# First modulation by slices of 128 output features, woven into the first two up tiles

## The reference

```python
def _rms(x, g):
    xf = x.astype(jnp.float32)
    y = xf * lax.rsqrt(jnp.mean(xf * xf, axis=-1, keepdims=True) + EPS)
    return y.astype(x.dtype) * g

def _modulate(xn, shift, scale):
    return xn * (1.0 + scale) + shift

def _swiglu(xm, w_in, w_out):
    a, u = jnp.split(xm @ w_in, 2, axis=-1)
    return (jax.nn.silu(a) * u) @ w_out
...
        ml = (jax.nn.silu(c) @ ada_w[l] + ada_b[l]).reshape(B, N_MOD, 1, D)
        mc = (jax.nn.silu(c_ctx) @ ada_w[l] + ada_b[l]).reshape(N_MOD, 1, 1, D)
        x = x + 0.5 * ml[:, 2] * _swiglu(_modulate(_rms(x, ffn1_norm[l]), ml[:, 0], ml[:, 1]), ffn1_w_in[l], ffn1_w_out[l])
        h = h + 0.5 * mc[2] * _swiglu(_modulate(_rms(h, ffn1_norm[l]), mc[0], mc[1]), ffn1_w_in[l], ffn1_w_out[l])
```

## Time and profile before

| | |
|---|---|
| median of 3 runs | 2353.45 us (2352.1 to 2355.32) |
| the profiled execution's own time | 2351.35 us |
| its span | 2349.6 us |
| TensorE busy | 2305.8 us, 98% |
| VectorE, ScalarE busy | 1577.8 us, 1143.3 us |
| DMA | 403.60 MB, mean 172 GB/s |

### The profile page before, as it was taken

How to read it: one execution, slowest core, us unless ns; L and a number is a source line. 1 busy time by engine, 2 the same in 40 slices (tenths; PEclk the granted TensorE clock), 3 DMA queues, 4 the chain that set the end, 5 groups by cost and what they waited for, 6 DMA issues and landing times.

```text
span 2349.6 us, 34192 instructions
## 1 busy us (share of the span) xinstructions
PE 2305.8 (98%) x13974; PEld 1942.9 (83%) x13974; DVE 1577.8 (67%) x2399; ACT 1143.3 (49%) x1692; POOL 24.4 (1%) x65
## 2 busy tenths in 40 slices
PE   7999999999999999999999999999999999999998
PEld 4887887888888787888888987888888888888887
DVE  4677433657665777667776678676676676876766
ACT  4222233446534355445545468654464455875544
POOL 0001000010000000000000000000000000000000
PEclk9999999999999999999999999999999999999999
DMA  7468322433522234654555544445545554434553
GB/s 308 179 232 323 143 90 90 153 116 145 192 91 73 75 122 159 239 190 169 196 219 194 209 147 146 157 179 190 187 179 198 217 206 180 157 140 177 183 196 125
DMA packets 59316, 403.60 MB, mean 172 GB/s; under 512 B 8269, under 2 KB 8805, under 8 KB 11672
## 3 DMA queue, kind: packets, MB, share of 16 engines
q1 hardware_dynamic: 52992, 384.33, 44.5%
q10 hardware_dynamic: 3840, 9.20, 1.1%
q0 software_dynamic: 2336, 7.96, 1.0%
HBM read 400.37 MB, written 2.67 MB: 172 GB/s over the span
## 4 chain that ended last, share of the span: by engine, by line
PE 90%; DVE 5%; ACT 2%; DMA 1%; issue 1%; SPq 0%; ACTq 0%; DVEq 0%
PE pair L558 86%; DVE ring_parts L2444 1%; PE pair L968 1%; DMA ring<-in_stream 1%; PE pair L656 1%; PE pair L1124 1%; PE pair L917 1%; ACT arena L2030 0%; DVE rows L2566 0%; ACT xT L1602 0%; DVE arena L3006 0%; PE pair L956 0%; DVE X L2572 0%; DVE xT_parts L2359 0%; ACT mix_high L1672 0%
## 5 line engine op out<-in xcount | busy, mean ns | idle before, releaser
L558 PE MATMUL pair<-xT_parts,ring_high 128*128 128x512 f32 x2112 | 747.5, 395 | 4.6 <-DVE xT_parts L2346 2.0
L558 PE MATMUL pair<-xT_parts,ring_parts 128*128 128x256 f32 (+2 forms) x2448 | 692.8, 298 | 1.4 <-DVE xT_parts L2359 1.4
L2432 DVE TENSOR_TENSOR ring_parts<-ring,ring_high 128x2048 fp32r<-128x2048 f32 x195 | 444.2, 2281 | 137.9 <-ACT ring_high L1659 137.7
L558 PEld LDWEIGHTS pair<-xT_parts,ring_parts 128*128 128x128 f32 (+1 forms) x2448 | 460.4, 188 | 41.4 <-issue 7.7
L558 PEld LDWEIGHTS pair<-xT_parts,ring_high 128*128 128x128 f32 x2112 | 384.5, 188 | 81.9 <-issue 2.8
L1659 ACT ACTIVATE ring_high<-ring 128x2048 fp32r<-128x2048 f32 x197 | 375.6, 1910 | 66.9 <-DMA ring<-in_stream 66.8
L1710 ACT ACTIVATE arena<-pair 128x512 f32<-128x512 f32 x110 | 65.6, 596 | 263.6 <-PE pair L558 263.6
L2444 DVE TENSOR_TENSOR ring_parts<-ring,mix_high 128x1024 fp32r<-128x1024 f32 x144 | 169.1, 1217 | 32.4 <-ACT mix_high L1672 32.2
L1672 ACT ACTIVATE mix_high<-ring 128x1024 fp32r<-128x1024 f32 x144 | 143.3, 1048 | 69.2 <-DMA ring<-in_stream 65.9
L558 PE MATMUL pair<-ring_parts,xT_parts 128*128 128x512 f32 (+1 forms) x448 | 174.0, 388 | 1.8 <-DVE ring_parts L2444 1.5
L558 PE MATMUL pair<-ring_parts,g_high 128*128 128x512 f32 x440 | 172.2, 391 | 0.2 <-issue 0.2
(11 more groups left out here) (441 smaller groups left out, 3837.3 us busy)
## 6 DMA issues: line engine op xcount, KB each, us to landing
ring<-in_stream SPq DMA_DIRECT2D x330, 1024.0 KB, 4.8
xn<-in_mods SPq DMA_DIRECT2D x14, 1024.0 KB, 4.9
arena<-in_mods SPq DMA_DIRECT2D x14, 1024.0 KB, 4.9
arena<-in_compress SPq DMA_DIRECT2D x8, 1024.0 KB, 6.8
gateB<-gate_rows POOLq DMA_DIRECT2D x4, 512.0 KB, 8.2
xn<-maximum_rows POOLq DMA_DIRECT2D x8, 256.0 KB, 3.6
arena<-in_bT ACTq DMA_DIRECT2D x1, 1536.0 KB, 9.3
bias_scratch<-bias_row POOLq DMA_DIRECT2D x1, 1536.0 KB, 8.9
```

Of the source, the lines that this page charges most:

```text
L558: m = pe.matmul(o, l, r, start=start, stop=stop)
L2432: ins = dve.tensor_tensor(out=ring_r[:, slot].rearrange("p a b -> p (a b)")[:, cols], in0=w[:, cols], in1=high[:, slot, cols], op=ALU.subt ...
```

## The change

The modulation weights are laid out anew: slice k (1 MB) holds, for all 1024 inputs, shift and scale of the 128 features of block k, so a feature block is done as soon as its slice is in. The eight slices no longer pass the ring; they have places of their own in the arena, in xn and in the ring's high parts. SP's queue loads x, ctx, slice 0, chunks 0 and 1, slices 1 to 7, chunks 2 and 3. For each slice TensorE does eight products of 256 columns over four groups of 32 partitions (the k blocks summed in fours), VectorE copies the result, and two products with `pick` (three additions of identity pieces) sum the four groups and bring them onto partitions; bias and gain are applied by two small VectorE operations. The rows are scaled by 1/rms ahead of the turning (`rooted_rows`), so the turning is a plain transpose. Up tiles 0 and 1 run slice by slice, both on the same feature block, with the next slices' products, transposes and picks between. Squares are over whole rows of 1024. Ahead of all this TensorE does 24 products of 64 x 64 constants (`awake`). The wait `FIRST_CONSTS` covers four loads (cT, ident, gains, biasM); the square-root table is loaded right behind the Silu; the bias rows and the clearing of their places go behind the first tile. Semaphores that became superfluous are merged (masks; the last rows' step).

```diff
+        rooted_rows = gateB
+        slices = [room(2048 * k, KD, S) for k in range(4)] + [
+            room(18 * N, KD, S), xn[:, :, :].rearrange("p a (b c) -> p (a b) c", c=S),
+            room(17408 + 2 * CW * N, KD, S), room(17408 + 3 * CW * N, KD, S)]
...
-            for j in range(SLOTS):
+            def first_load(j):
                 sp.dma_start(ring[:, j], t["stream"][j]).then_inc(loaded[j], 16)
-            turns, whole = NCH // SLOTS, (QUAD + MOD_STEPS + 2) // SLOTS + 1
+            def slice_load(k):
+                sp.dma_start(slices[k], t["slices"][k]).then_inc(slice_in[k][0], 16)
+            sp.dma_start(X[:, 0:2, :], t["x"]).then_inc(inputs, 16)
+            sp.dma_start(X[:, 2:4, :], t["ctx"]).then_inc(ctx_in, 16)
+            slice_load(0)
+            first_load(0)
+            first_load(1)
+            for k in range(1, 6):
+                slice_load(k)
+            for j in range(2):
+                sp.wait_ge(loaded[j], 16)
+                slice_load(6 + j)
+            for j in range(2, 4):
+                sp.wait_ge(loaded[j], 16)
+                first_load(j)
+            sp.wait_ge(mod_full, 6)
+            sp.dma_start(mod_w[0], t["mods"][0]).then_inc(aside_loaded[0], 16)
+            turns, whole = NCH // SLOTS, (MOD_STEPS + 2) // SLOTS + 1
             for n in range(SLOTS, SLOTS * whole):
                 sp.wait_ge(read[n % SLOTS], n // SLOTS)
                 sp.dma_start(ring[:, n % SLOTS], t["stream"][n]).then_inc(loaded[n % SLOTS], 16)
-                f = n - QUAD - 3
+                f = n - 3
                 for m in mod_chunks(f) if f >= 0 else ():
                     if m >= 2:
                         sp.wait_ge(aside_read[m % 2], m // 2)
+                    else:
+                        sp.wait_ge(mod_full, 5)
...
+            def slice_products(k):
+                pe.wait_ge(*slice_in[k])
+                if k >= 2:
+                    pe.wait_ge(mod_row, k - 1)
+                at = k % 2 * S
+                for kd in range(KD):
+                    g = kd % 4
+                    mm(bank[4][32 * g:32 * g + 32, at:at + S], scT[:, kd, :], slices[k][:, kd, :], kd < 4, kd >= 4,
+                       mod_full if kd == KD - 1 else None)
+            def slice_turn(k):
+                if k >= 2:
+                    pe.wait_ge(x_whole, k - 1)
+                for t_ in range(4):
+                    if k == 0:
+                        pe.wait_ge(rstd_done, t_ + 1)
+                    m = pe.transpose(bank[6 + k % 2][:, t_ * P:(t_ + 1) * P], rooted_rows[:, t_, k * P:(k + 1) * P],
+                                     ident[:, :])
+                m.then_inc(x_turned, 1)
+            def slice_pick(k):
+                pe.wait_ge(mod_row, k + 1)
+                for m in range(2):
+                    mm(bank[5][:, 4 * k + 2 * m:4 * k + 2 * m + 2], modrow[:, k % 2, m * P:(m + 1) * P], pick, True, True,
+                       mod_turned if m else None)
+            def awake(n):
+                pe.wait_ge(zeroed, 1)
+                for _ in range(n):
+                    mm(bank[7][0:64, 0:64], unit, unit, True, True)
             def modulation():
+                awake(AWAKE)
                 pe.wait_ge(consts, FIRST_CONSTS)
                 pe.wait_ge(sc_done, 1)
-                for k in range(KD):
-                    if k == KD - 2:
-                        norm_wide(range(0, 2))
-                    chunk_wait(c.chunk)
-                    quad_part(0, k, ring[:, c.chunk % SLOTS], mod_full if k == KD - 1 else None)
-                    owed.append(read[c.chunk % SLOTS])
-                    c.chunk += 1
-                quad_turn(0)
+                slice_products(0)
+                slice_turn(0)
+                pe.wait_ge(zeroed, 3)
+                slice_pick(0)
...
+                def up_slice(k):
+                    pe.wait_ge(x_split, k + 1)
+                    for f in range(2):
+                        if k % CW == 0:
+                            pe.wait_ge(low_ready, 2 * (k // CW) + f + 1)
+                        up_steps(f, f, [(half, range(k, k + 1)) for half in range(2)])
+                        if k == KD - 1:
+                            owed.append(read[(c.chunk + f) % SLOTS])
+                def slices_start():
+                    up_slice(0)
+                    for k in (1, 2):
+                        slice_products(k)
+                        slice_turn(k)
+                        slice_pick(k)
+                    for k in range(3, KD):
+                        slice_products(k)
+                        slice_turn(k)
+                        up_slice(k - 2)
+                        slice_pick(k)
+                    up_slice(KD - 2)
+                    up_slice(KD - 1)
...
             act.dma_start(cT[:, :, :], t["cT"]).then_inc(consts, 16)
             act.dma_start(ident[:, :], t["ident"]).then_inc(consts, 16)
-            act.dma_start(X[:, 0:2, :], t["x"]).then_inc(inputs, 16)
-            act.dma_start(X[:, 2:4, :], t["ctx"]).then_inc(inputs, 16)
+            act.dma_start(gains[:, :, :], t["gains"]).then_inc(consts, 16)
+            act.dma_start(biasM, t["biasM"]).then_inc(consts, 16)
             def modulation():
                 act.wait_ge(consts, FIRST_CONSTS)
-                act.wait_ge(zeroed, 1)
+                act.wait_ge(zeroed, 2)
                 act.activation(scT[:, :, 0:2], cT[:, :, :], ACT.Silu).then_inc(sc_done, 1)
-                act.dma_start(gains[:, :, :], t["gains"]).then_inc(more_consts, 16)
-                act.wait_ge(zeroed, 3)
+                sqrt_table()
...
+            def first_norm():
+                act.wait_ge(var_done, 4)
+                for t_ in range(4):
+                    if t_ % 2 == 0:
+                        act.wait_ge(ctx_in if t_ else inputs, 16)
+                    c.squares += 1
+                    if t_ >= 2:
+                        act.wait_ge(squares, c.squares - 2)
+                    act.activation(whole_junk[:, t_ % 2, :], X[:, t_, :], ACT.Square, scale=D ** -0.5,
+                                   accum_out=ss[:, 1, t_:t_ + 1]).then_inc(squares, 1)
+                    c.sd += 1
+                    act.wait_ge(squares, c.squares)
+                    act.activation(sd[:, t_:t_ + 1], ss[:, 1, t_:t_ + 1], ACT.Sqrt,
+                                   bias=var[:, t_:t_ + 1]).then_inc(sd_done, 1)
...
+            def slice_out(k):
+                c.turned += 1
+                act.wait_ge(x_turned, k + 1)
+                act.wait_ge(mod_done, k + 1)
+                for half in range(2):
+                    cols = slice(half * S, (half + 1) * S)
+                    ins = act.activation(xTl[:, k, cols], bank[6 + k % 2][:, cols], ACT.Identity,
+                                         bias=modT[:, k, half:half + 1], scale=normA[:, half, k:k + 1])
+                ins.then_inc(x_whole, 1)
+            def slices_out():
+                first_half_high(0, 0)
+                slice_out(0)
+                first_half_high(1, 0)
+                first_half_high(0, 1)
+                slice_out(1)
+                first_half_high(1, 1)
+                for k in range(2, KD - 1):
+                    slice_out(k)
+                act.wait_ge(mod_full, KD)
+                split(0, 2)
+                slice_out(KD - 1)
...
...
+                dve.memset(scT[:, :, :], 0.0).then_inc(zeroed, 1)
+                dve.memset(var[:, 0:4], EPS).then_inc(var_done, 4)
+                dve.wait_ge(consts, FIRST_CONSTS)
+                step(dve.tensor_tensor(out=pick, in0=ident[:, 0:2], in1=ident[:, 32:34], op=ALU.add))
+                step(dve.tensor_tensor(out=pick, in0=pick, in1=ident[:, 64:66], op=ALU.add))
+                dve.tensor_tensor(out=pick, in0=pick, in1=ident[:, 96:98], op=ALU.add).then_inc(zeroed, 1)
+                step(dve.tensor_scalar(biasM[:, 1, :], biasM[:, 1, :], 1.0, None, ALU.add))
+            def first_norm():
+                c.squares += 4
+                for t_ in range(4):
+                    c.sd += 1
+                    dve.wait_ge(sd_done, c.sd)
+                    step(dve.reciprocal(rstd[:, t_:t_ + 1], sd[:, t_:t_ + 1]))
+                    dve.tensor_scalar(rooted_rows[:, t_, :], X[:, t_, :], rstd[:, t_:t_ + 1], None,
+                                      ALU.mult).then_inc(rstd_done, 1)
+            def slice_row_out(k):
+                dve.wait_ge(mod_full, k + 1)
+                if k >= 2:
+                    dve.wait_ge(mod_turned, k - 1)
+                dve.tensor_copy(modrow[:, k % 2, 0:S], bank[4][:, k % 2 * S:(k % 2 + 1) * S]).then_inc(mod_row, 1)
+            def slice_keep(k):
+                dve.wait_ge(mod_turned, k + 1)
+                dve.tensor_scalar(modT[:, k, :], bank[5][:, 4 * k:4 * k + 2], biasM[:, 0, k:k + 1], None, ALU.add)
+                dve.tensor_scalar(normA[:, 0:2, k], bank[5][:, 4 * k + 2:4 * k + 4], biasM[:, 1, k:k + 1],
```

(27 more changed lines are left out.)

174 lines of the change are left out of this document (93 added, 81 removed).

## The result

The changed kernel took 2358.27 us (median of 17 runs, 2356.41 to 2360.62), the kernel before 2352.72 (17 runs, 2349.57 to 2355.32): 5.55 us more, a ratio of 1.0024 with a 95% interval of 1.0018 to 1.0031. That is slightly slower, just over the 0.2% that the prediction set as the bound of "no change" (the interval holds 0.2% too), and inside its range. The profiled execution took 2357.29, its span is 2355.5.

What follows compares the result with a forecast made beforehand. TensorE, busy 98% of 2349.6 us, bounds the kernel. 27.2 + 34.6 + 2.3 + 2.0 = 66.1 puts the step of 62.80 at 66.3, +3.5 us; on the median 2353.45 that gives 2357.0, range 2350 to 2361.

Steps and rivals of the forecast that it cites:

- When the consts land: Start: four small loads pass one packet for each large one, 2.7 us per load; all in at 14.3, not 8.9.
- To the first up product: From Silu's end at 14.6 through table, squares, scaling, transposes and slice 0: first up product at 27.2, against 40.72.
- Both tiles: Up tiles 0 and 1 after 27.2: 34.6 us of work, 2.3 of stalls, 2.0 of clock loss, ending at 66.1.
- the 34.6: TensorE's work in both tiles: up slices 21.8, modulation products 6.7, transposes 2.9, picks 3.2 us.
- The clock at the start: First up slices: TensorE starts at 1.2 GHz, 4 us at half pace, a loss of 2.0 us; bounds 0 and 3.4.
- The start as a whole: Second up tile's sigmoid-linear step moves from 62.80 to 66.3: +3.5 us, taken as the change's whole effect.
- Everything behind it is the same work in the same order.: From the third up tile to the end: nothing changes, so the shift at the start is the whole effect.
- the bound of 4.7: Whole time: a measurement tells 0.2%, 4.7 us, from no change; smaller shifts count as "no change".
- They cost nothing (hidden by the wait for the consts) and I give them nothing.: The 24 constant products ahead of the modulation, some 6 us from about 1.5: zero cost and zero gain.
- Rival 1: Between up slices 0 and 1 the clock falls once more: slower, 2358.7 to 2362, 2360 taken; chance 0.32.
- Rival 2: Start: all four small loads in by 6 us, tiles end at 57.9, 2348.5; chance of gain over 4.7 us 0.12.
- Rival 3: Start: the constant products do hold the clock, shift +1.5, 2355, no change; within the 0.56 left.

Runs made afterwards that it cites:

- those in the holes: Changed kernel plus constant products: 4 ahead of each of slice 0's transposes 2 to 4, 12 behind its pick; 2358.93 us, ratio 1.0031.
- the small loads ahead: Changed kernel with cT, ident, gains and biasM issued on SP's queue ahead of x, no longer on ScalarE's queue; 2350.84 us, ratio 0.9991.

## Why the prediction was right, and where not

- **When the consts land.** Right: 14.3 was forecast, the Silu starts at 14.03. One packet for one: from 9 to 10 us of the changed kernel SP's queue moved 51 packets and ScalarE's 54. Removing two loads gave 5.4 us, as summed. The Trainium skill (DMA: Bandwidth & Descriptors, Queues, rings and completion order), by which a small load would pass in a turn, disagrees with these counts and with the landing times of 9.6 and 11.8 us.
- **To the first up product.** 27.2 forecast, 26.47 measured. A row tile takes 1.37, not 1.44; the last root ends at 21.22 (21.9), the last transpose at 22.7 (23.1), the pick takes 0.98 at the low clock (0.9).
- **Both tiles.** 39.6 us from the first up product to the third tile, 38.9 forecast, by luck in its parts. The products came to 1.7 more than the 34.6: an up slice took 2.85 and not 2.72, a slice of modulation products 1.0 and not 0.96, and the transposes and picks of slices 1 and 2 1.15 where 0.87 was summed. The stops came to 1.8 and not 2.3: 1.0 ahead of up slice 7 (1.3 taken), 0.4 ahead of the pick of slice 2 (of the 1.0), and the 0.3 ahead of the third tile that no term held.
- **The clock at the start.** 4 us at half pace forecast, 3.2 measured (26.47 to 29.67), so some 1.5 us lost and not 2.0. The clock rose at 5.78 under the constants and fell at 9.19, before slice 0, as reckoned. The Trainium skill (TensorE: Matmul & The Clock Gate, What's actually happening) has the low clock as the default, which activity lifts and idleness brings back; this trace agrees. It also varies: 29.67 and 31.77 in two profiles of one kernel.
- **The start as a whole.** +3.5 forecast, +3.5 measured (66.06 against 62.60). The path and its waits were right; that the total agrees to 0.1 is luck: 0.7 early at the first up product, 0.5 and 0.5 less for stops and clock, against 1.7 more for the products. A second profile of the same kernel gave +4.5. The step that the forecast went by, the silu of the second tile, came at 66.89, not 66.3 (+4.1): ScalarE had begun the split of a chunk (1.9 us) ahead of it. TensorE didn't wait for it.
- **"Everything behind it is the same work in the same order."** This step failed. It is the same work, but 2.0 us were lost in it, which alone carried the time over the bound of 4.7. In the pair of profiles it was 1.4 by three pauses, which stand at the borders between pieces of 256 instructions, moved by 41 by the change, and 0.8 by falls of the clock, whose places vary. So the likeliest class, "no change", was missed by little, and the middle of the range, 2357.0, by 1.3 us.
- **"They cost nothing (hidden by the wait for the consts) and I give them nothing."** Half wrong. Where they run, this holds: with 0, 24 or 80 of them the first up product doesn't come sooner. But they move the pauses near 685 and 795 us: their number changed the time by 4.1 us in the changed kernel where both were timed on one chip (24 against none, in its favour; 6.4 to 7.4 by the second run, from medians of two chips) and by 4.1 in the kernel before (against it).
- **Rivals.** Rival 1 had the size (2358.7 to 2362) with another cause: no fall came between up slices 0 and 1. Falls come later, at pauses, in the kernel before as well. Rival 2 didn't happen; in the form "issue them first" it was made to happen, and gave 5.8 us at the start and 6.0 in the median, each against the kernel before beside it. Rival 3: the constants ahead didn't hold the clock; those in the holes did, for 1.5.

What stays open: what makes the clock fall at a given pause in one execution and not in the next; why the pauses of one kernel differ by up to 0.55 between executions, and why the one near 795 is only 0.52 with the small loads ahead, at the same border. No run removed the small products' bursts, and none added 128 full-precision records (256 instructions with their weight loads), which by the count should leave every pause as it is.

## What to carry to other kernels

A small load of 128 rows issued beside a busy queue costs one large packet per row, 2.7 us here however few its bytes: issue what the first instruction waits for ahead of the large loads, and wait for no more than that instruction reads. On an engine that is busy 98% of the time, "hidden under a wait" isn't yet "free": instructions added anywhere shift where its supply runs dry in later bursts of tiny ones, so compare the pauses without a releaser in both traces, count TensorE's instructions up to each, and vary the number of padding instructions before a result of 0.2% is put down to the edit's idea. Take the shift of one and the same instruction along the whole span: it separates a start, a pause and a fall of the clock at once.

## What was not expected of the hardware

- Pauses of TensorE of 0.4 to 2.9 us in bursts of records of 0.01 us, with a 16 KB instruction packet landing 1.25 to 1.61 us before their end, and each at the same place of a piece of 256 TensorE instructions. Their length goes with where in the burst that border lies (near 685 us 0.67 in the kernel before, 2.92 with 48 more records ahead).
- A single pause of 1 to 3 us in otherwise unbroken work can be followed by a stretch at 0.50 of the clock of 3.4 or 6.8 us, worth 1.3 to 1.6 us for the shorter, and need not be: at the same pause near 411 us the clock fell in one profile of the kernel before and not in the other.
